# Three unit places moved by unused gaps in SBUF, in an fp32 kernel of ten stages

## The reference

```python
def swiglu(u, w1, w2):
    gate, up = jnp.split(u @ w1, 2, axis=-1)
    return (jax.nn.silu(gate) * up) @ w2

hid = silu(ragged_dot(xs, w_gate, sizes)) * ragged_dot(xs, w_up, sizes)   # the experts
y = ragged_dot(hid, w_down, sizes)
```

## Time and profile before

| what | us |
|---|---|
| median of 3 runs | 3172.99 (3172.69 to 3173.51) |
| span of the profiled execution | 3172.4 |
| PE, matmuls | 3136.1, 99% of the span, 15857 instructions |
| PE, weight loads (beside the matmuls) | 2611.5, 82% |
| DVE | 2219.9, 70% |
| ACT | 1871.5, 59% |
| chain of waits | PE 93%, DVE 4%, ACT 2% |
| DMA | 730 MB, 230 GB/s in the mean |

### The profile page before, as it was taken

One profiled execution on the slowest core, in us unless ns is written; L12 is line 12 of the kernel. 1 busy time (PEld: TensorE's weight loads), 2 busy tenths in 40 slices (PEclk: granted clock), 3 DMA queues, 4 the chain that ended last, 5 costly groups with the idle time before them and its releaser, 6 DMA issues.

```text
span 3172.4 us, 39857 instructions
## 1 busy us (share of the span) xinstructions
PE 3136.1 (99%) x15857; PEld 2611.5 (82%) x15857; DVE 2219.9 (70%) x2626; ACT 1871.5 (59%) x2487; POOL 48.8 (2%) x67
## 2 busy tenths in 40 slices
PE   9999999999999999999999999999999999999998
PEld 7888588888887878988888889887888888888887
DVE  5559865655445566665754757667999999999998
ACT  5442554544455444655544457465777777777777
POOL 1000000000000000000000000000000000000000
PEclk9999999999999999999999999999999999999999
DMA  9444274665536444535374545346999999999995
GB/s 326 145 168 145 92 234 150 201 204 166 140 107 219 146 160 160 186 134 185 124 235 138 181 161 194 123 153 226 384 376 382 382 376 382 382 376 382 381 377 225
DMA packets 383079, 730.39 MB, mean 230 GB/s; under 512 B 13027, under 2 KB 152689, under 8 KB 382784
## 3 DMA queue, kind: packets, MB, share of 16 engines
q1 hardware_dynamic: 376576, 705.87, 62.4%
q0 software_dynamic: 6224, 22.16, 2.3%
q10 hardware_dynamic: 112, 0.05, 0.0%
HBM read 720.16 MB, written 7.86 MB: 229 GB/s over the span
## 4 chain that ended last, share of the span: by engine, by line
PE 93%; DVE 4%; ACT 2%; issue 0%; DMA 0%; DVEq 0%; SPq 0%; ACTq 0%
PE duo L1075 14%; PE duo L1077 14%; PE duo L1076 14%; PE acc L1075 8%; PE acc L1077 8%; PE acc L1076 8%; PE aux L1075 2%; PE aux L1076 2%; PE aux L1077 2%; PE aux L553 1%; PE duo L554 1%; PE duo L553 1%; PE aux L554 1%; PE duo L555 1%; PE aux L555 1%; PE duo L398 1%
## 5 line engine op out<-in xcount | busy, mean ns | idle before, releaser
L1741 DVE TENSOR_TENSOR weights_split<-w,weights_split 128x1024 fp32r<-128x1024 f32 x672 | 792.5, 1221 | 80.2 <-ACT weights_split L1717 78.9
L1717 ACT ACTIVATE weights_split<-w 128x1024 fp32r<-128x1024 f32 x672 | 675.3, 1053 | 205.4 <-PE duo L1077 128.3
L1075 PE MATMUL duo<-weights_split,u_high 128*128 128x512 f32 x1776 | 698.7, 393 | 1.2 <-issue 0.8
L1077 PE MATMUL duo<-weights_split,u_low 128*128 128x512 f32 x1776 | 692.6, 390 | 0.0
L1076 PE MATMUL duo<-weights_split,u_high 128*128 128x512 f32 x1776 | 692.0, 390 | 0.0
L427 DVE TENSOR_TENSOR w_low<-w,w_high 128x1024 fp32r<-128x1024 f32 x304 | 368.2, 1223 | 291.0 <-ACT w_high L418 289.6
L1220 DVE TENSOR_TENSOR weights_split<-w,weights_split 128x1024 fp32r<-128x1024 f32 x320 | 377.2, 1221 | 268.4 <-ACT weights_split L1208 268.2
L418 ACT ACTIVATE w_high<-w 128x1024 fp32r<-128x1024 f32 x304 | 318.2, 1057 | 315.1 <-PE acc L1077 80.2
L1208 ACT ACTIVATE weights_split<-w 128x1024 fp32r<-128x1024 f32 x320 | 320.7, 1054 | 239.3 <-PE duo L1077 139.9
L1075 PEld LDWEIGHTS duo<-weights_split,u_high 128*128 128x128 f32 x1776 | 333.7, 188 | 71.6 <-issue 3.7
L1077 PEld LDWEIGHTS duo<-weights_split,u_low 128*128 128x128 f32 x1776 | 333.5, 188 | 70.2
(11 more groups left out here) (448 smaller groups left out, 4954.8 us busy)
## 6 DMA issues: line engine op xcount, KB each, us to landing
w<-in_ffn_w_dram SPq DMA_DIRECT2D x130, 1024.0 KB, 7.8
w<-in_moe_w_gate_dram SPq DMA_DIRECT2D x112, 1024.0 KB, 8.1
w<-in_moe_w_up_dram SPq DMA_DIRECT2D x112, 1024.0 KB, 7.9
w<-in_moe_w_down_dram SPq DMA_DIRECT2D x112, 1024.0 KB, 9.6
w<-in_w_in_dram SPq DMA_DIRECT2D x92, 1024.0 KB, 7.2
w<-in_hyb_w_in_dram SPq DMA_DIRECT2D x18, 1024.0 KB, 8.2
w<-in_ffn_w_gate_dram SPq DMA_DIRECT2D x11, 1024.0 KB, 7.6
w<-in_ffn_w_up_dram SPq DMA_DIRECT2D x11, 1024.0 KB, 10.1
```

The lines of the kernel that those rows point to most:

```text
L1075: pe.matmul(bank_out, x_hi, w_hi, start=first, stop=False, skip_group_check=True)
L1077: return pe.matmul(bank_out, x_lo, w_hi, start=False, stop=last, skip_group_check=True)
L1717: act.activation(units[:, place, 0, cut], src[:, cut], ACT.Copy).then_inc(sem("moe_high"), 1)
L1741: m = dve.tensor_tensor(units[:, place, 1, cut], src[:, cut], units[:, place, 0, cut], ALU.subtract)
```

## The change

The tensor `weights_split` becomes three tensors, place_a, place_b and place_c, with an unused gap ahead of each: 48, 32 and 32 float32 numbers, which is 192, 128 and 128 bytes. With the activations (u_low, u_high, hidden_T_split) at 0 within 512 bytes, the places then begin at 192, 320 and 448. What lies behind them (hidden_T_odd, arena_rest, con, par, small) moves on by 448 bytes in all. The arena grows by the 112 numbers, and `view` adds the gaps to offsets at or beyond a place. To make room `small` shrinks from 440 to 424 columns, and decay_tot, 16 columns that nothing reads, goes. Every `units[:, x, ...]` becomes `places[x][:, ...]`. No instruction, wait, order or transfer is added or taken away.

```diff
-        with nc.sbuf_tensor("arena", [P, ARENA], F32) as arena:
+        PLACE_GAPS = (48, 32, 32)
+        PLACES_AT = (8192, 12288, 16384)
+        with nc.sbuf_tensor("arena", [P, ARENA + sum(PLACE_GAPS)], F32) as arena:
             pass
...
-        units = sb("weights_split", [P, 3, 2, 2048], F32R)
+        places = []
+        for n, gap in enumerate(PLACE_GAPS):
+            sb(f"place_gap{n}", [P, gap])
+            places.append(sb(f"place_{'abc'[n]}", [P, 2, 2048], F32R))
...
-        small = sb("small", [P, 440])
+        small = sb("small", [P, 424])
...
             assert off + n <= ARENA, (off, shape)
+            off += sum(gap for gap, at_place in zip(PLACE_GAPS, PLACES_AT) if off >= at_place)
             v = arena[:, off:off + n]
...
-        decay_tot = cols(16)
...
-                    whi, wlo = (units[:, x, y, :].rearrange("p (t n) -> p t n", n=COLS) for y in range(2))
+                    whi, wlo = (places[x][:, y, :].rearrange("p (t n) -> p t n", n=COLS) for y in range(2))
...
-                act.activation(units[:, place, 0, cut], src[:, cut], ACT.Copy).then_inc(sem("moe_high"), 1)
+                act.activation(places[place][:, 0, cut], src[:, cut], ACT.Copy).then_inc(sem("moe_high"), 1)
...
-                m = dve.tensor_tensor(units[:, place, 1, cut], src[:, cut], units[:, place, 0, cut], ALU.subtract)
+                m = dve.tensor_tensor(places[place][:, 1, cut], src[:, cut], places[place][:, 0, cut], ALU.subtract)
```

More of the change, by code:

```diff
@@ L221, in cols @@
             used[0] += n
-            assert used[0] <= 440
+            assert used[0] <= 424
             return small[:, used[0] - n:used[0]]
@@ L1154, in down @@
                     pe.wait_ge(sem("hidT_split"), hidT0 + j + 2 + body * i)
-                whi, wlo = (units[:, 1 if last else 2, y, :].rearrange("p (t n) -> p t n", n=D) for y in range(2))
+                whi, wlo = (places[1 if last else 2][:, y, :].rearrange("p (t n) -> p t n", n=D) for y in range(2))
                 x = hidden_at(j)
@@ L1207, in act_unit @@
                 cut = slice(1024 * piece, 1024 * (piece + 1))
-                act.activation(units[:, x, 0, cut], src[:, cut], ACT.Copy).then_inc(sem(f"unit_hi{x}"), 1)
+                act.activation(places[x][:, 0, cut], src[:, cut], ACT.Copy).then_inc(sem(f"unit_hi{x}"), 1)
         def dve_unit(key, x, i, n, body, pieces=(0, 1)):
@@ L1219, in dve_unit @@
                 dve.wait_ge(sem(f"unit_hi{x}"), ev.base(f"unit_hi{x}", key) + 2 * n + piece + 1 + 2 * body * i)
-                m = dve.tensor_tensor(units[:, x, 1, cut], src[:, cut], units[:, x, 0, cut], ALU.subtract)
+                m = dve.tensor_tensor(places[x][:, 1, cut], src[:, cut], places[x][:, 0, cut], ALU.subtract)
             if 1 in pieces:
@@ L1232, in act_last_unit @@
                 cut = slice(1024 * piece, 1024 * (piece + 1))
-                act.activation(units[:, 1, 0, cut], src[:, cut], ACT.Copy).then_inc(sem("unit_hi2"), 1)
+                act.activation(places[1][:, 0, cut], src[:, cut], ACT.Copy).then_inc(sem("unit_hi2"), 1)
         def dve_last_unit(key, total):
@@ L1241, in dve_last_unit @@
                 dve.wait_ge(sem("unit_hi2"), ev.base("unit_hi2", key) + 2 * (total - 1) + piece + 1)
-                m = dve.tensor_tensor(units[:, 1, 1, cut], src[:, cut], units[:, 1, 0, cut], ALU.subtract)
+                m = dve.tensor_tensor(places[1][:, 1, cut], src[:, cut], places[1][:, 0, cut], ALU.subtract)
             m.then_inc(sem("unit_split2"), 1)
@@ L1618, in up @@
                         pe.wait_ge(sem("moe_low"), j + 1)
-                    whi, wlo = (units[:, place, y, :].rearrange("p (t n) -> p t n", n=COLS) for y in range(2))
+                    whi, wlo = (places[place][:, y, :].rearrange("p (t n) -> p t n", n=COLS) for y in range(2))
                     for k in range(4):
@@ L1636, in down @@
                     place = down_place(j, last)
-                    whi, wlo = (units[:, place, y, :].rearrange("p (t n) -> p t n", n=D) for y in range(2))
+                    whi, wlo = (places[place][:, y, :].rearrange("p (t n) -> p t n", n=D) for y in range(2))
                     for half in range(2):
@@ L2491, in build @@
         oB = u[:, 0:4, :].rearrange("p a b -> p (a b)").rearrange("p (t n) -> p t n", n=512)
-        oBh = units[:, 2, 1, 512:1536].rearrange("p (c t) -> p c t", t=T)
+        oBh = places[2][:, 1, 512:1536].rearrange("p (c t) -> p c t", t=T)
         oBl = hT[:, :, :, :].rearrange("p a b t -> p (a b) t")
@@ L2694, in build @@
         merged = view(0, NT, D)
-        cFh, cFl = (units[:, 0, y, :].rearrange("p (c t) -> p c t", t=T) for y in range(2))
+        cFh, cFl = (places[0][:, y, :].rearrange("p (c t) -> p c t", t=T) for y in range(2))
         ro = view(4096, NT, D)
@@ L3310, in build @@
         wP = [view(18944 + 1024 * i, 1024) for i in range(2)]
-        mBh, mBl = (units[:, 2, y, :].rearrange("p (c t) -> p c t", t=T) for y in range(2))
+        mBh, mBl = (places[2][:, y, :].rearrange("p (c t) -> p c t", t=T) for y in range(2))
         wo = view(4096, NT, D)
```

## The result

| kernel | median, us | range | span of the profiled execution |
|---|---|---|---|
| before | 3172.84 | 3172.65 to 3173.51 | 3172.4 |
| changed | 3208.99 | 3208.39 to 3209.04 | 3206.6 |

The ratio is 1.011 (95% interval 1.0098 to 1.0122): 36 us slower, where 11.7 us less were forecast. The time lies in the range of the second rival, the slower one (3189 to 3215).

The account below looks back on a forecast made before the run. PE was taken as the bound: number of matmuls by the distance between starts. Places a -10.4, b -5.6 and c +4.3 gave -11.7 us; 3172.4 - 11.7 + 0.6 = 3161.3 us, 8 in 10 from 3115 to 3200.

Parts of the forecast that it names:

- Rival 2: Split products: 0 is the best distance for 512 columns, others pay 2.2 to 5.7 ns; 3189 to 3215 us, chance 0.29.
- What bounds it: Whole kernel: time is the number of PE matmuls by the distance between starts, 226.7 ns for a split product.
- For a I take the positive row, -3.9: Place a, +192: priced by 256-column matmuls at +64 and +128, -3.9 ns on 2664 products, -10.4 us.
- lead 0: Moving operand's place less the stationary one's, within 512 bytes, is 0; every split product before, at 226.7 ns.
- For b the middle between that and 0, -2.0: Place b, +320 or -192: midway between place a's -3.9 and 0, -2.0 ns on 2784 products, -5.6 us.
- c +2.2 by its own row: Place c at -64: priced by 512-column products at -64 and -128, +2.2 ns on 1932 products, +4.3 us.
- The upper end, 5.7: Products at -64 and -128: 5.7 ns more each by mean busy times, partly first products after a break.
- The bound from below (-10.9, 215.8): Places a and b: a product can gain at most 10.9 ns, reaching the unhindered 215.8.
- c with hidden_T_odd stays: Place c against hidden_T_odd: both move to +448, so 612 products keep their distance and price.
- Rest of the edit at 0: DVE and ACT work, units as stationary operand (528 products, about ±1 us), moved constants and small: 0.
- Rival 1: Split products: every distance costs the same, a weight load meeting the moving read once; no change, 3173 us, chance 0.23.

Follow-up runs that it names:

- p1: Computation left out, products alone, moving operand 0 to 496 bytes beyond the stationary one: settled 226.7 ns at 0, 233.3 at 192 and 448, 228.9 at 320.
- p2: Computation left out, products alone with finer distances, narrower operands, repeated moving bytes, or two distances in turn: 228.9 ns for -64 and -128 in turn, 215.8 for 16 repeated bytes.
- e4: Kernel before with all three places and hidden_T_odd moved by 256 bytes: 3174.35 us, ratio 1.0001.
- e1: Kernel before with only place a moved, to 192 bytes: 3195.23 us, ratio 1.0065.
- e2: Kernel before with only place b moved, to 320 bytes: 3188.00 us, ratio 1.0042.
- e3: Kernel before with only place c moved, to 448 bytes, hidden_T_odd kept at 0: 3193.38 us, ratio 1.0059.
- p5: Computation left out, runs of 96 products alternating pieces at two distances: 0 with 192 bytes took 22.49 us by threes, 22.35 by 48.
- p6: Computation left out, stretches of 72 products in blocks of 8 numbers every 32, with different breaks between: each settled at 220.0 or 230.4 to 230.8 ns.
- v4: Kernel before with dense FFN units read in blocks of 4 numbers every 16, at 64 bytes, and experts' units at 256: 3163.26 us, ratio 0.9964.
- p3: Computation left out, products alone with either operand moved, one-column weights, bf16 or other reading orders: 220.0 ns for 8 numbers with hops of 32, 215.8 for bf16.

## Why the prediction was wrong

- **What bounds it: right.** The time moved with the distance between the starts of the split products, 32.4 of the 33.0 us. The counts of the moved products were as said, and ACT's pieces kept their times (1052 and 1054 ns above against 1053).
- **"For a I take the positive row, -3.9": the step that failed.** It measured +6.3: +16.7 us in the sum where it had -10.4. The earlier trace rows are of 256 columns and were compared with 108.8, and their 7.0 ns over that was set against the 10.9 of 512 columns. p1 shows what was missing: at 256 columns lead 0 is the dearest (120.0), at 512 the cheapest (226.7). A price taken from one length of stream did not carry to another. And it was the wrong row: with a period of 256 bytes a's +192 is c's -64, so the two places have one price (233.3 in p1), where the prediction gave them -3.9 and +2.2.
- **"For b the middle between that and 0, -2.0": wrong by the same step**, and measured at +1.9: +5.2 us for -5.6. That +320 is also -192 was noted; that it is also +64 was not, since the circle was taken to be 512 bytes, the length of one slice of weights.
- **"c +2.2 by its own row": the sign right, the size wrong**, +5.4 measured: +10.4 us for +4.3. The earlier trace rows have two leads, -64 for w_high and -128 for w_low, in one chain, and products of two leads in turn have a price of their own: 228.9 in p2, where -64 alone has 233.3. The upper end, 5.7 from the groups' busy times, holds the result by luck: it contains the first products behind breaks, and the settled distance of that mixture is +2.2 (p2).
- **The bound from below (-10.9, 215.8) exists**, but not by lead: bf16 and 16 repeated bytes reach it, and none of the leads tried does.
- **c with hidden_T_odd stays: right** (+0.1 us on 612 products).
- **Rest of the edit at 0: right in e4.** The turned products, though, whose operands don't move, took 3.4 us more (118.0 against 116.5 ns); e1 has 2.4 of it and e2 and e3 nothing, so it came mostly with place a, where cF stands in a mixer. Part may be chance: the kernel before, too, has 1.0 us more than e4 here. By what p5 and p6 show a changed neighbour could do this; no run isolates it. The products with a unit as the stationary operand are 800, not 528 (w_low moves in another 272); they moved by less than 1 us in all.
- **Rival 2 was the mechanism, its range right in part by luck.** 16.7 + 5.2 + 10.4 = 32.3 us on 7380 products are 4.4 ns each, inside its 2.2 to 5.7. That lead 0 is the best of those tried came true; that each other place pays as -64 does didn't (6.3, 1.9 and 5.4 ns), and the 5.7 is no settled price of the earlier trace rows. What spoke for it was the only direct comparison in the trace: 512 columns at lead 0 against 512 columns at another. It should have outweighed the row of another shape.
- **Rival 1** argued that a full stretch of 512 bytes meets the other read once, wherever it begins. e4 shows this at 256, and every other lead shows that it isn't so. The Trainium skill ("TensorE: Matmul & The Clock Gate", Part 2, "Step-by-step") has two independent read ports, by which no lead would matter. The runs have 226.7 to 240.0 by the distance of the two operands alone. For bf16 they agree with it: 215.8 at all four leads.

Not settled: why an fp32r product takes more than the bare 215.8 at all, how the place of the stationary operand comes into it, and what decides which state a break leaves. The runs give only the prices.

## What to carry to other kernels

Where the distance between matmul starts is steady and yet above the bare stream, the number may be a settled state of the reads, and not a constant: price an edit of places by a row of the same length, type and order of reading, or by a small kernel that sweeps the distance, before trusting a trend from another shape. The place where every split product already sits at lead 0 is worth keeping, and moving one tensor out of three also disturbs the one that is read next. A better price was had by the order in which the moving operand is read (v4), and it had to be tried behind the kernel's own breaks, since an unbroken run (p3's 220.0) promised 26 us and gave 3.

## What was not expected of the hardware

- 512 columns of fp32r cost 226.7 to 240.0 ns a matmul by the distance between moving and stationary operand, with a period of 256 bytes; as bf16 215.8 at each of four distances.
- With one column read 128 times as the weights, or with only 2 columns, the price at lead 0 is 231.7, above the 226.7 with all 128.
- The order in which the moving columns are read takes it from 220.0 (8 numbers, hops of 128 bytes) to 277.4 (4 numbers, hops of 256 bytes) and 431 (2 numbers, hops of 64 bytes), while ACT's copies and DVE's subtractions into the orders tried (8 numbers with hops of 128 bytes, 4 with hops of 64) take what they take in natural order (612 to 613 and 682 to 691 ns for 512 numbers).
- One and the same stream of matmuls has two lasting speeds, 220.0 and 230.7 ns, and can change from one to the other at a break of 0.6 us, though the same break doesn't always leave the same one.
